# Early modulation of a two-layer denoising step: one quarter ahead of the weight products, three beside them

## The reference, cut to what matters

```
shift, scale, gate = split(silu(cond) @ w_ada + b_ada, 3)   # w_ada: 2048 x 6144
h = rmsnorm(x, g) * (1 + scale) + shift
q, k, v, z = split(h @ w_in, 4)                             # w_in: 2048 x 8192
...
x = x + gate * ((attention(q, k, v) * silu(z)) @ w_out)
```

## Time and profile before

| what | value |
|---|---|
| median of three runs | 1168.44 us |
| profiled execution | 1168.6 us, its span 1166.8 us |
| PE busy | 1095.3 us (94%) |
| weight loads of PE | 826.0 us (71%) |
| DVE, ACT, POOL busy | 756.3, 570.3, 216.0 us |
| moved by DMA | 325.04 MB |
| mean PE clock granted | 0.971 of full speed |

### The profile page before, as it was taken

How to read it: one execution, slowest core, us unless ns; L and a number is a source line. 1 busy time by engine, 2 the same in 40 slices (tenths; PEclk the granted TensorE clock), 3 DMA queues, 4 the chain that set the end, 5 groups by cost and what they waited for, 6 DMA issues and landing times.

```text
span 1166.8 us, 17367 instructions
## 1 busy us (share of the span) xinstructions
PE 1095.3 (94%) x6786; PEld 826.0 (71%) x6786; DVE 756.3 (65%) x1208; ACT 570.3 (49%) x801; POOL 216.0 (19%) x378
## 2 busy tenths in 40 slices
PE   3799999999999999999999989999898998999995
PEld 0265777676777777778767657888686876888884
DVE  4145765766665765667687776369966895476564
ACT  5233434434434444345443346566768486455443
POOL 2001230343113411222133431100020202100000
PEclk9788999999999999999999999999898998999998
DMA  9999687888879987876598877877472867864551
GB/s 361 420 411 409 243 293 268 332 335 334 314 277 381 354 332 271 333 271 213 236 380 335 334 257 284 272 234 249 149 259 103 265 225 251 304 232 159 204 186 72
DMA packets 64114, 325.04 MB, mean 279 GB/s; under 512 B 9409, under 2 KB 16193, under 8 KB 32033
## 3 DMA queue, kind: packets, MB, share of 16 engines
q1 hardware_dynamic: 43904, 265.98, 61.4%
q0 software_dynamic: 12944, 46.94, 11.5%
q10 hardware_dynamic: 7184, 11.01, 2.6%
HBM read 295.55 MB, written 28.34 MB: 278 GB/s over the span
## 4 chain that ended last, share of the span: by engine, by line
PE 74%; DVE 9%; DMA 7%; ACT 6%; issue 3%; SPq 0%; POOL 0%; DVEq 0%; ACTq 0%; POOLq 0%
PE ps L803 19%; PE ps L804 18%; PE ps L805 18%; PE ps L677 6%; DMA araw<-in_wada 4%; DVE wlo L1468 3%; DMA raw<-in_w 2%; ACT whi L1069 2%; PE ps L912 2%; PE ps L935 1%; PE ps L786 1%; PE ps L735 1%; PE ps L752 1%; DVE sb L1586 1%; ACT hy L1181 1%
## 5 line engine op out<-in xcount | busy, mean ns | idle before, releaser
L1468 DVE TENSOR_TENSOR wlo<-raw,whi 128x1024 fp32r<-128x1024 f32 x288 | 351.8, 1226 | 289.6 <-ACT whi L1069 285.6
L1069 ACT ACTIVATE whi<-raw 128x1024 fp32r<-128x1024 f32 x288 | 302.9, 1058 | 429.5 <-PE ps L805 408.5
L803 PE MATMUL ps<-whi,xhi 128*128 128x512 f32 x1152 | 471.1, 409 | 3.7 <-DVE wlo L1468 2.3
L804 PE MATMUL ps<-wlo,xhi 128*128 128x512 f32 x1152 | 454.0, 394 | 0.0
L805 PE MATMUL ps<-whi,xlo 128*128 128x512 f32 x1152 | 453.6, 394 | 0.0
L803 PEld LDWEIGHTS ps<-whi,xhi 128*128 128x128 f32 x1152 | 219.3, 190 | 87.6 <-issue 28.4
L805 PEld LDWEIGHTS ps<-whi,xlo 128*128 128x128 f32 x1152 | 218.8, 190 | 48.5
L804 PEld LDWEIGHTS ps<-wlo,xhi 128*128 128x128 f32 x1152 | 219.5, 191 | 41.3
L677 PE MATMUL ps<-araw,cT 128*32 128x512 f32 x640 | 83.1, 632 | 7.3 <-DMA araw<-in_wada 7.3
L677 PEld LDWEIGHTS ps<-araw,cT 128*32 128x32 f32 x640 | 16.5, 111 | 50.5 <-issue 27.4
L619 POOL DMA_DIRECT2D ctab<-ctab_scratch x16 | 8.6, 541 | 189.7 <-PE ps L935 189.7
(11 more groups left out here) (209 smaller groups left out, 1068.3 us busy)
## 6 DMA issues: line engine op xcount, KB each, us to landing
raw<-in_w SPq DMA_DIRECT2D x144, 1024.0 KB, 5.7
araw<-in_wada SPq DMA_DIRECT2D x80, 1024.0 KB, 8.7
raw<-in_wada SPq DMA_DIRECT2D x16, 1024.0 KB, 9.2
ctab_scratch<-ce POOLq DMA_DIRECT2D x16, 512.0 KB, 7.2
btab_scratch<-bs ACTq DMA_DIRECT2D x32, 256.0 KB, 4.8
btab<-btab_scratch SPq DMA_DIRECT2D x16, 512.0 KB, 3.9
ctab<-ctab_scratch POOLq DMA_DIRECT2D x16, 512.0 KB, 5.2
par<-in_par POOLq DMA_DIRECT2D x32, 128.0 KB, 6.2
```

The costliest lines, as they stand in the source:

```text
L803: mm(acc, xhi[:, kt, st], whi[:, s, k], start=kt == 0, stop=False)
L804: mm(acc, xhi[:, kt, st], wlo[:, slot, k0 % 2, k], start=False, stop=False)
L1069: af(whi[:, k % 4].rearrange("p k c -> p (k c)"), src, ACT.Copy).then_inc(s_hi, 1)
L1468: tt(wlo[:, slot, k % 2].rearrange("p k c -> p (k c)"), src, whi[:, k % 4].rearrange("p k c -> p (k c)").bitcast(F32), ALU.subtract).then_ ...
```

## The change

Only quarter 0 is ahead of unit 0. Quarter 1 has its chunks behind units 0 to 3, quarter 2 behind 4 to 7, quarter 3 behind 8 to 11. The loads on SP are reordered: the pieces for units 0 to 3 stand behind chunk 3, the piece for units 4 and 5 behind chunk 13, and so on. The first three table quarters move to later units. The waits for the banks they share with attention move with them: the transposes of table quarter 2 now stand behind unit 25 and wait for `scores_shifted` 3. Four constants (`ident`, `sel2`, `bT`, `gT`) are loaded from ACT's queue, and only `condT` from SP's, ahead of the chunks. The number of instructions that compute is the same.

The core of the diff:

```diff
@@ table_units: units of the first three table quarters
-        return ((3, 9, 6, 11, 12), (11, 14, 14, 19, 20), (17, 21, 20, 27, 28))[n]
+        return ((3, 12, 6, 14, 15), (14, 19, 17, 21, 22), (20, 25, 22, 27, 28))[n]
@@ SP: constants, loads
-            for name, dst in (("condT", condT), ("ident", ident),
-                              ("sel2", sel2), ("bT", bT), ("gT", gT)):
-                sp.dma_start(dst[:], d[name]).then_inc(s_const, 16)
+            sp.dma_start(condT[:], d["condT"]).then_inc(s_condin, 16)
-                for e in {0: range(0, 16), 2: range(16, 24), 4: range(24, 32)}.get(g, ()):
+                for e in {0: range(4), 2: range(4, 14), 3: range(14, 16), 4: range(16, 22), 5: range(22, 24), 6: range(24, 32)}.get(g, ()):
@@ PE: waits of the tables and of attention
+                                if n == 1:
+                                    pe.wait_ge(s_kTsb, 2)
+                                if n == 2:
+                                    pe.wait_ge(s_sub, 3)
-                                if n < 12 and n % 3 == 2:
+                                if 3 <= n < 12 and n % 3 == 2:
                                     pe.wait_ge(s_kTsb, 2 * (n // 3 + 1))
...
-                    pe.wait_ge(s_bs, 2 * (3 * hb + 1) if hb else 4)
+                    pe.wait_ge(s_bs, 2 * (3 * hb + 1))
...
-                    pe.wait_ge(s_bs, 2 * (3 * hb + 3))
+                    if hb == 0:
+                        pe.wait_ge(s_bandd, 2)
+                    pe.wait_ge(s_bs, 2 * (3 * hb + 3) if hb else 4)
@@ PE: order at the start
             for j in range(0, 2 * NCK, 2):
                 ada_early(0, j)
-            for j in range(0, NCK, 2):
-                ada_early(1, j)
             early_columns(0)
             early_tiles(0)
-            for j in range(NCK, 2 * NCK, 2):
-                ada_early(1, j)
-            early_columns(1)
-            early_tiles(1)
...
-                if k < 8:
-                    c = k // 4 + 2
+                if k < 12:
+                    c = k // 4 + 1
                     ada_early(c, k % 4 * 2)
@@ ACT (DVE has the same but for adasb_early)
+            for name, dst in (("ident", ident), ("sel2", sel2), ("bT", bT), ("gT", gT)):
+                act.dma_start(dst[:], d[name]).then_inc(s_const, 16)
...
             adasb_early(0, 0)
+            for k in range(4):
+                split(k)
             adasb_early(0, 1)
             early_tiles(0)
-            adasb_early(1, 0)
-            adasb_early(1, 1)
-            split(0)
-            split(1)
-            early_tiles(1)
-            split(2)
-            split(3)
...
-                if k < 8 and k % 4 == 3:
+                if k < 12 and k % 4 == 3:
                     split(k + 1)
                     split(k + 2)
-                    early_tiles(k // 4 + 2)
+                    early_tiles(k // 4 + 1)
                     split(k + 3)
                     split(k + 4)
```

More of the change, by code:

```diff
@@ L685, in ada_columns @@
                 return last
-            pe.wait_ge(s_const, 16 * 5)
+            pe.wait_ge(s_const, 16 * 4)
             pe.wait_ge(s_cond, 1)
@@ L694, in ada_early @@
                     half, part = i // NCK, i % NCK
-                    if part == 0 and c >= 2:
-                        pe.wait_ge(s_adasb, 2 * c + half if half else 1 if c == 2 else 2 * c)
+                    if part == 0 and c >= 1:
+                        pe.wait_ge(s_adasb, 2 * c + half if half else 1 if c == 1 else 2 * c)
                     src, landed = early_slot(8 * c + i)
@@ L740, in tables @@
                         pe.wait_ge(s_bs, 2 * n + 1)
-                        if n == 1:
-                            pe.wait_ge(s_kTsb, 2)
-                        if n < 12 and n % 3 == 2:
+                        if 3 <= n < 12 and n % 3 == 2:
                             pe.wait_ge(s_sub, 3 * (n // 3 + 1))
@@ L843, in attention @@
                     pe.wait_ge(s_bandd, 3 * hb + 3)
+                    if hb == 0:
+                        pe.wait_ge(s_bs, 6)
                     for i in range(3):
@@ L1238, in _ @@
                         high(i, g)
-                if 8 <= k < NU - 4 and k != UB * B_IN1 - 1:
+                if 12 <= k < NU - 4 and k != UB * B_IN1 - 1:
                     split(k + 4)
@@ L1249, in _ @@
                 s5_beside(k)
-                if k < 8 and k % 2 == 1:
-                    adasb_early(k // 4 + 2, k // 2 % 2)
-                if k < 8 and k % 4 == 3:
+                if k < 12 and k % 2 == 1:
+                    adasb_early(k // 4 + 1, k // 2 % 2)
+                if k < 12 and k % 4 == 3:
                     split(k + 1)
                     split(k + 2)
-                    early_tiles(k // 4 + 2)
+                    early_tiles(k // 4 + 1)
                     split(k + 3)
```

6 lines of the change are left out of this document (3 added, 3 removed).

## The result

The changed kernel takes 1190.62 us, the median of four runs (1186.08 to 1190.69), against 1168.58 for the kernel before, measured beside it. The ratio is 1.0185, with an interval of 1.0166 to 1.0205: slower by 22.0 us. Forecast were 1176 us, slower by 7.7. The direction and most of the mechanisms came as forecast, the size was nearly three times as large.

The account below looks back on a forecast made before the run. The prediction took the load stream to bound the start and PE the rest. It summed +5.7 us at the seam up to unit 12, -4.1 at table quarter 1 and +6.1 at table quarter 2 to +7.7: 1176 us, range 1168 to 1184.

Parts of the forecast that it names:

- the wait at table quarter 1: PE's 2.55 us wait ahead of these transposes and its 1.5 us restart were to go: -4.1 us.
- the wait of 4.79 us at table quarter 2: Behind unit 25 PE was to wait 4.6 us for DVE's softmax subtraction; with a 1.5 us restart, +6.1 us.
- Rival 1: The load stream still decides the start: unit 12 at 112.9, 12.5 us earlier; total 1161.5 us; chance 0.08.
- Rival 2: Quarter boundaries stay at 4.7 us, tiles finished while PE transposes; 1168.5 us, no change; chance 0.12.
- Rival 3: The softmax wait at table quarter 2 doesn't come, DVE ahead of PE in loop 24; 1170 us; chance 0.13.
- Rival 4: Low clock holds as long as at 109.35 at all five restarts, +1.5 us each; 1184 us; chance 0.17.
- Unit 12: Step dating unit 12 from unit 0's start, three quarters of 28.2 us and late chunks: 127.6 against 125.35, 2.3 us later.
- The start of unit 0: With 8 chunks ahead instead of 16, unit 0 was to start at 42.7 us, 16 us earlier.
- 0.3 in all: Late chunk loads up to unit 12: only each quarter's last chunk late by a tenth or two, 0.3 us in all.
- The restarts: PE restarting at 1.2 GHz behind a thin stretch loses 1.5 us each time, bounds 0.4 and 3.0.
- The boundaries: Ahead of units 4, 8 and 12, last chunk to fresh tile takes 7.3 us each; PE fills 4.7, idles 2.6.
- From unit 12 to unit 28: Table quarter 0's leftover +1.9, restart at unit 12 +1.5, table quarter 1 -4.1, table quarter 2 +6.1 us.

Follow-up runs that it names:

- a_oldtile: Changed kernel, but units 4 to 15 multiply the activation tiles of quarter 0 and don't wait for their own; 1180.28 us, ratio 1.0112.
- b_constact_late: Kernel before, with four constants on ACT's queue and PE waiting for them only ahead of the first columns; 1167.7 us, ratio 1.0.
- a_t0late: Changed kernel, with DVE's and POOL's part of table quarter 0 moved from units 3 to 7 to units 8 to 12; 1184.07 us, ratio 1.0144.
- a_six: Changed kernel with six slots for chunks instead of four; 1182.98 us, ratio 1.0132.
- b_t15: Kernel before, with table quarter 1 transposed one unit later, behind units 15 and 16; 1165.33 us, ratio 0.9978.
- a_constsp: Changed kernel with all five constants issued by SP ahead of the chunks, as before; 1191.04 us, ratio 1.0195.
- a_mended: Changed kernel with six slots, SP's queue reordered, fillers (useless PE transposes), DVE's tiles first, table quarters 0 and 2 later; 1170.13 us, ratio 1.0016.

## Why the prediction was right in direction and wrong in size

**What came as forecast.** The three waits for `xlo`, with DVE as the releaser (2.79, 2.10 and 4.81 us for 2 to 3 each); the end of the wait at table quarter 1; the wait of 4.79 us at table quarter 2 (4.6 forecast); DMA shares of 0.70, 0.87 and 0.74 in the quarters, so the stream does pause, though it is full in the boundaries (1.01 and 1.02); chunk 7 at 36.20 (35.3) and unit 0 at 44.25 (42.7), 14 us earlier than before. None of that came through to the end, since unit 12 is what counts. Rival 1 (the stream decides, faster) fell: the windows of the quarters add up to more than their loads take. Rival 2 (boundaries of 4.7) fell as well. a_oldtile makes its premise true, units 4 to 15 starting right behind the transposes, and gives back 8.5 to 10.3 us. Rival 3 fell with the wait of 4.79. Rival 4, the clock, was partly true: the restarts cost 2.1 to 2.8 us where it had 3.0 and the sum 1.5. One of the forecast's own signs of being wrong came true as well, chunk loads waited for in units 0 to 11: 3.7 us.

**The step that failed is "Unit 12".** It gave 127.6, and it was 137.64, 10.0 us off; about two thirds of all that was missing. Its terms, from the windows above:

- The start of unit 0: 44.25 for 42.7, 1.5 us. Chunk 7 started 0.9 us late (36.20 for 35.3): of the 1.5 us given to the constants, 0.7 shows in the stream (its seventh megabyte is used at 28.72, before at 29.44), and b_constact_late has nothing of it in the total. The other 0.6 lie between chunk 7 and the first `xlo`: the chunk took 1.93 us at the low clock, 0.9 more than a fast one, and I had added 0.3.
- "0.3 in all" for late chunks. The waits in the quarters are 0.44 and 1.37 + 1.89 = 3.26 us, 3.4 more. My walk from slot to slot had a load land 4.7 us after its issue, as in a queue nearly empty. Chunks 22 and 23, issued from 84.79 on, the last two of five megabytes issued since 80.00, took 9.9 and 12.0 us. In a_t0late, with the same issue times and without table quarter 0 in that stretch, they took 8.4 and 10.0. I had also not asked what stands ahead of a chunk in SP's queue; that held the two up in a_six, not in the changed kernel.
- The restarts, 1.5 each. A quarter's window less 19.36 and less its chunk waits gives 2.1, 2.8 and 2.7: 7.6 for 4.5, 3.1 more. The mean of four unlike rows (0.4 to 3.0) was too kind. Directly ahead of the two cheap ones PE had stood still for 0.8 us each, ahead of the other two for 1.75 and 2.55, and the restarts behind the new waits for `xlo` (2.1 to 2.8 us within the quarters) are of the second sort. a_oldtile, which has no such wait at units 4 and 8, gives 2.4 and 1.4 where the changed kernel has 2.8 and 2.7. So the idle time is part of the price, not all of it.
- The boundaries, 7.3 each: 24.0 for 21.9, 2.1 more. The first was right (7.25). In the second the columns took 3.54 us instead of 1.92, at the low clock behind the late chunks. In the third nothing of PE's own was slow. There the chain started late: ACT waited 1.12 us for a weight piece, ahead of the splits that stand ahead of the tiles. From there to `xlo` it ran as in before's rows:

```profile
130.96 2.00 ACT L1066 ACTIVATE whi<-raw 128x1024 fp32r<-128x1024 f32 x2 [1.12 <-DMA raw<-in_w]
```

```profile
132.05 2.36 DVE L1459 TENSOR_TENSOR wlo<-raw,whi 128x1024 fp32r<-128x1024 f32 x2 [20.42 <-ACT whi L1066]
...
136.89 0.69 DVE L1478 TENSOR_TENSOR xlo<-ps,xhi 128x512 fp32r<-128x512 f32 x1 [0.72 <-ACT xhi L1088]
```

These are the timelines of ACT and DVE in the changed kernel, `whi`, `wlo` and `xlo` of units 12 and 13. 1.5 + 3.4 + 3.1 + 2.1 is 10.1. It has to be the miss at unit 12 but for rounding, since the windows share out the whole stretch; the causes rest on the runs. The four terms are coupled: behind the late chunk 23 the clock was low, and at the low clock the columns took longer.

**From unit 12 to unit 28** the forecast has 1.9 + 1.5 - 4.1 + 6.1 = 5.4 us, and it was 8.4. Unit 12 at 0.50 and the following 5 us at 0.92 cost 2.7 + 0.4 = 3.1 instead of 1.5. The softmax wait and its restart are 4.8 + 5.35 x 0.43 = 7.1 instead of 6.1. The wait at table quarter 1 that went may have given back less than 4.1, and b_t15 doesn't settle it (0.5 to 4.7). The 1.9 is a small slip, 16.0 - 4 x 2.8 - 3.0 is 1.8. The last 1.3 us behind unit 28 are unexplained.

**The range** (1168 to 1184) missed since I had a rival for dear restarts alone (1184 us), and none in which chunks, boundaries and restarts go wrong together. The Trainium skill ("TensorE: Matmul & The Clock Gate", section "HAM oscillation — how this bites in real kernels") had said that work cut into bursts pays the low clock at each burst. The windows agree: 0.91, 0.89, 0.86. By that rule all restarts are of the dear kind, and I had given it 0.17.

## What to carry to other kernels

Starting PE earlier gained nothing here, and will gain nothing where the order behind it makes each later step wait for a fresh result: count the chain at every boundary, and add the restart at the low clock and the effect of one late load. When loads are walked through by slots, don't give each the landing time of an empty queue: count what was issued shortly before it, other queues' stores too, and what SP holds ahead of it. A mended order that comes level with the old one has not shown that the idea is good: ask what the same mends would do for the old one.

## What the runs showed of the hardware that was not expected

Small loads issued beside the large ones landed late. `gT`, issued by SP at 2.59 us ahead of all chunks, landed in 2.0 us; issued by ACT at 2.14, with chunks already in flight, it took 14.5 (the landing of tile `gT`, before and after):

```profile
DMA to landing us min/median/max: 2.0/2.0/2.0
```

```profile
DMA to landing us min/median/max: 14.5/14.5/14.5
```

`ident`, first on ACT's queue, took 2.0, `sel` and `bT` took 5.8 and 9.9 us, each later one longer. b_constact_late has the same for `gT` (14.7), and a_constsp, with SP issuing them ahead of the chunks again, 2.2. Whether the place behind the chunks or ACT's queue matters more wasn't separated. The Trainium skill ("DMA: Bandwidth & Descriptors", section "Issuing engines are not separate DMA queues") has the engines shared by all issuers, and the runs agree; by it a second issuing queue saves issuing time only, and here the small loads paid for it with 12 us of landing.

The columns, 16 matmuls of 128x2, did not bring the clock back. Behind a late chunk they took 3.54 us instead of 1.92, and the tile transposes behind them still ran low, 1.95 instead of 1.07. With 27 more transposes of 128x128 around them, and nothing late, a_mended went through the later boundaries with the clock whole (1.00 in its windows from 73.78 on).
